# Feed-forward up projections of a two-layer block: two of the three partial products in one 512-column matmul, the sum formed afterwards

## The reference, cut to what matters

```
def conv_ffn(h, w_up, conv_w, conv_b, w_down):
    u = h @ w_up                                   # (256, 1024) @ (1024, 8192)
    u = causal depthwise conv of u, 3 taps, + conv_b
    gate, val = jnp.split(u, 2, axis=-1)
    return (jax.nn.gelu(gate, approximate=True) * val) @ w_down
```

## Time and profile before

| what | value |
|---|---|
| median of three runs | 2301.82 us |
| the profiled execution's own time | 2301.09 us |
| its span in the trace | 2299.3 us |
| TensorE, matmuls, busy over the span | 2040.8 us, 89% |
| VectorE busy | 1628.1 us, 71% |
| ScalarE busy | 1147.3 us, 50% |

### The profile page before, as it was taken

One profiled execution on the slowest core, in us unless ns is written; L12 is line 12 of the kernel. 1 busy time (PEld: TensorE's weight loads), 2 busy tenths in 40 slices (PEclk: granted clock), 3 DMA queues, 4 the chain that ended last, 5 costly groups with the idle time before them and its releaser, 6 DMA issues.

```text
span 2299.3 us, 30590 instructions
## 1 busy us (share of the span) xinstructions
PE 2040.8 (89%) x10162; PEld 1354.8 (59%) x10162; DVE 1628.1 (71%) x3313; ACT 1147.3 (50%) x2527; POOL 850.2 (37%) x574
## 2 busy tenths in 40 slices
PE   9999999999999899987778788999899987778887
PEld 8998899998999744432223233998754432223222
DVE  4564777776776787777677776776787767677776
ACT  5454455555454555544444445455555544444453
POOL 0000011100010256566666663020265566666664
PEclk9999999999999999999999999999999999999999
DMA  7543466665535799999999999534799999999997
GB/s 245 167 127 119 138 188 203 199 188 194 178 112 178 279 421 421 421 421 421 421 421 419 422 422 370 176 120 166 266 421 421 421 421 422 421 420 422 422 422 323
DMA packets 120993, 710.39 MB, mean 309 GB/s; under 512 B 14016, under 2 KB 14272, under 8 KB 54720
## 3 DMA queue, kind: packets, MB, share of 16 engines
q0 software_dynamic: 76992, 546.34, 57.5%
q1 hardware_dynamic: 41744, 151.60, 20.5%
q10 hardware_dynamic: 2160, 11.17, 1.2%
HBM read 708.02 MB, written 4.19 MB: 310 GB/s over the span
## 4 chain that ended last, share of the span: by engine, by line
PE 43%; DMA 24%; POOL 9%; issue 8%; DVE 7%; ACT 7%; DVEq 0%; POOLq 0%; ACTq 0%
DMA work<-in_experts,expert_idx 24%; PE ps L477 10%; PE ps L478 10%; PE ps L479 10%; POOL work L988 9%; PE ps L1174 7%; PE ps L615 2%; DVE work L1865 2%; DVE weights_lo L462 2%; PE ps L593 1%; PE ps L583 1%; ACT L1461 1%; ACT weights_hi L457 1%; ACT L1407 1%; ACT arena L1466 1%
## 5 line engine op out<-in xcount | busy, mean ns | idle before, releaser
L1174 PE MATMUL ps<-work,arena 128*128 128x512 f32 x2048 | 1002.5, 623 | 216.0 <-ACT arena L1466 215.0
L988 POOL DMA_INDIRECT work<-in_experts,expert_idx x512 | 798.2, 1559 | 591.9 <-PE ps L1174 306.3
L1174 PEld LDWEIGHTS ps<-work,arena 128*128 128x128 f32 x2048 | 365.1, 193 | 828.8 <-ACT arena L1466 523.3
L1865 DVE CUSTOM_DVE_ANT_0 work<-h_norm,work 128x1024 f32<-128x1024 f32 x480 | 588.1, 1225 | 309.8 <-DMA work<-in_experts,expert_idx 305.7
L462 DVE TENSOR_TENSOR weights_lo<-weights,weights_hi 128x1024 fp32r<-128x1024 f32 x286 | 354.7, 1245 | 180.9 <-ACT weights_hi L457 179.9
L477 PE MATMUL ps<-feat_hi,weights_hi 128*128 128x256 f32 x1576 | 459.6, 292 | 9.2 <-DVE weights_lo L462 5.8
L457 ACT ACTIVATE weights_hi<-weights 128x1024 fp32r<-128x1024 f32 x286 | 301.7, 1057 | 321.9 <-PE ps L479 288.3
L1461 ACT ACTIVATE small<-small 128x1 f32<-128x1 f32 x512 | 150.2, 293 | 606.6 <-DVE small L1865 585.4
L478 PE MATMUL ps<-feat_lo,weights_hi 128*128 128x256 f32 x1576 | 446.7, 283 | 0.0
L479 PE MATMUL ps<-feat_hi,weights_lo 128*128 128x256 f32 x1576 | 446.5, 283 | 0.0
L477 PEld LDWEIGHTS ps<-feat_hi,weights_hi 128*128 128x128 f32 x1576 | 303.0, 192 | 18.6 <-issue 9.0
(11 more groups left out here) (218 smaller groups left out, 1777.5 us busy)
## 6 DMA issues: line engine op xcount, KB each, us to landing
weights<-in_wstream SPq DMA_DIRECT2D x286, 512.0 KB, 3.8
work<-in_experts,expert_idx POOLq DMA_INDIRECT x512, 14.6
arena<-in_wstream POOLq DMA_DIRECT2D x12, 512.0 KB, 6.4
na_rows<-in_rpb POOLq DMA_DIRECT2D x32, 96.0 KB, 4.6
arena<-na_rows ACTq DMA_DIRECT2D x2, 1536.0 KB, 9.9
params<-in_par ACTq DMA_DIRECT2D x2, 1476.0 KB, 6.6
arena<-in_bias ACTq DMA_DIRECT2D x5, 512.0 KB, 4.9
params<-in_par ACTq DMA_DIRECT2D x1, 1024.0 KB, 6.4
```

The costliest lines, as they stand in the source:

```text
L988: nc.gpsimd.indirect_dma_start(ring[:, r, :], None, experts, bass.IndirectOffsetOnAxis(ap=EIDX[:, b, c * RING + r:c * RING + r + 1], axis= ...
L1174: ins = nc.tensor.matmul(bank(2 * t + h), DIAG[:, r, :], ring[:, r, D + h * 512:D + (h + 1) * 512], start=False, stop=False)
L1865: nc.vector.tensor_tensor_reduce(ring[:, r, 0:D], HN[:, t, :], ring[:, r, 0:D], 1.0, 0.0, ALU.mult, ALU.add, hd[:, r:r + 1]).then_inc(dots ...
```

## The change

High and low part of a chunk of features now lie side by side in one tensor (`FEAT`, of which `FH` and `FL` are views). `block_wide` issues two matmuls for a chunk: the high part of the weights against both parts of the features, 512 columns, and the low part of the weights against the high features, 256 columns, added to the second 256 columns of the first. A half so fills a bank of its own with two sums, and two blocks use banks 4 to 7. Behind them stand two new steps: ScalarE copies the second sums of a block to SBUF (`ff_copy_act`, 128 x 512), VectorE adds the first sums (`ff_sum_dve`, 128 x 512) into the tensor `ffu` in SBUF. The taps read `ffu` in place of PSUM, and TensorE waits for `ff_summed` where it waited for `ff_conv`. Elsewhere in the program only the access patterns of the feature parts change.

```diff
-        FH, FL = sb("feat_hi", [P, KC, S], F32R), sb("feat_lo", [P, KC, S], F32R)
+        FEAT = sb("feat", [P, KC, 2, S], F32R)
+        FH, FL = FEAT[:, :, 0, :], FEAT[:, :, 1, :]
...
+        ffu = work[:, 2048:3072].rearrange("p (j g n) -> p j g n", j=2, g=2)
...
+        def ff_parts(j, a):
+            return ps[:, (4 + 2 * j) * 512:(6 + 2 * j) * 512].rearrange("p (g a n) -> p g a n", g=2, a=2)[:, :, a, :]
+
+        def block_wide(pe, g, j, at=0, also=None):
+            for h in range(2):
+                w, out = split_pe(pe, 2 * g + h, at), bank(4 + 2 * j + h)
+                for c in range(KC):
...
+                    hi, lo = cols(w, c * P, P)
+                    nc.tensor.matmul(out, hi, FEAT[:, c, :, :].rearrange("p a n -> p (a n)"), start=c == 0, stop=False)
+                    ins = nc.tensor.matmul(out[:, S:2 * S], lo, FH[:, c, :], start=False, stop=c == KC - 1)
+                ins.then_inc(half_done, 1)
...
             with pe.Fori(0, FF_BLOCKS // 2 - 1) as i:
...
-                    pe.wait_ge(ff_conv, i * 2 + j + 1)
-                    group_fm(pe, G_FF + 2 + j, 6 + j, at)
+                    pe.wait_ge(ff_summed, i * 2 + j + 1)
+                    block_wide(pe, G_FF + 2 + j, j, at)
...
+            def ff_copy_act(j, done):
+                act.wait_ge(half_done, done)
+                nc.scalar.activation(ffu[:, j, :, :], ff_parts(j, 1), ACT.Copy).then_inc(ff_copied, 1)
+
             def ff_init_act(j, cvw, done):
-                act.wait_ge(half_done, done)
+                act.wait_ge(ff_summed, done)
                 for gv in range(2):
-                    ins = nc.scalar.activation(ffacc[:, j, gv, :], bank(6 + j)[:, gv * S:(gv + 1) * S], ACT.Identity,
+                    ins = nc.scalar.activation(ffacc[:, j, gv, :], ffu[:, j, gv, :], ACT.Identity,
                                                scale=cvw(gv, 2), bias=cvw(gv, 3))
...
                     split_hi(act, F_HALF + 7 + 2 * j, at)
+                    ff_copy_act(j, at.halves + F_HALF + 6 + 2 * j)
+                    split_hi(act, F_HALF + 8 + 2 * j, at)
                     act.wait_ge(ff_prod, i * 2 + j + 1)
-                    ff_init_act(j, taps, at.halves + F_HALF + 6 + 2 * j)
-                    split_hi(act, F_HALF + 8 + 2 * j, at)
+                    ff_init_act(j, taps, i * 2 + 3 + j)
                     ff_gelu_act(i * 2 + 2 + j, j)
...
+            def ff_sum_dve(blk, j):
+                dve.wait_ge(ff_copied, blk + 1)
+                nc.vector.tensor_tensor(ffu[:, j, :, :], ff_parts(j, 0), ffu[:, j, :, :], ALU.add).then_inc(ff_summed, 1)
...
                     split_lo(dve, F_HALF + 7 + 2 * j, at)
+                    ff_sum_dve(i * 2 + 2 + j, j)
+                    split_lo(dve, F_HALF + 8 + 2 * j, at)
                     ff_conv_dve(i * 2 + 2 + j, j, taps)
-                    split_lo(dve, F_HALF + 8 + 2 * j, at)
                     ff_gate_dve(i * 2 + 2 + j, j)
```

More of the change, by code:

```diff
@@ L250, in two, with paired_cols @@
         def two(t, b):
-            return t[:, 2 * b:2 * b + 2, :].rearrange("p c n -> p (c n)")
+            return t[:, 2 * b:2 * b + 2, :]
+        def paired_cols(ap):
+            return ap.rearrange("p (c n) -> p c n", c=2)
         x0_loaded, x1_loaded, ident_loaded, const_loaded, par1_loaded, bias_loaded = sem("x0_loaded"), sem("x1_loaded"), sem("ident_loaded"), sem("const_loaded"), sem("par1_loaded"), sem("bias_loaded")
@@ L276, in build @@
         ff_squared, ff_gained = sem("ff_squared"), sem("ff_gained")
+        ff_copied, ff_summed = sem("ff_copied"), sem("ff_summed")
         ff_init, ff_conv, ff_gelu, ff_gated = sem("ff_init"), sem("ff_conv"), sem("ff_gelu"), sem("ff_gated")
@@ L369, in norm_dve_pre @@
                 if gain_fm is None:
-                    ins = nc.vector.tensor_tensor(two(FL, b), bank(b), two(FH, b), ALU.subtract)
+                    ins = nc.vector.tensor_tensor(two(FL, b), paired_cols(bank(b)), two(FH, b), ALU.subtract)
                 else:
@@ L386, in norm_act_hi @@
                 if gain_fm is None:
-                    ins = nc.scalar.activation(two(FH, b), bank(b), ACT.Copy)
+                    ins = nc.scalar.activation(two(FH, b), paired_cols(bank(b)), ACT.Copy)
                 else:
@@ L499, in group_fm @@
                                       c == chunks[0], c == chunks[-1])
+                ins.then_inc(half_done, 1)
[5 more added lines that the diff above has]
+                for c in range(KC):
+                    if also and h == 0:
+                        also(c)
+                    hi, lo = cols(w, c * P, P)
+                    nc.tensor.matmul(out, hi, FEAT[:, c, :, :].rearrange("p a n -> p (a n)"), start=c == 0, stop=False)
+                    ins = nc.tensor.matmul(out[:, S:2 * S], lo, FH[:, c, :], start=False, stop=c == KC - 1)
                 ins.then_inc(half_done, 1)
@@ L695, in heads_parts @@
                 n = fill + f
-                src = bank(6 + f if f < EARLY else 4 + n % 2)
+                src = paired_cols(bank(6 + f if f < EARLY else 4 + n % 2))
                 if eng is nc.scalar:
@@ L770, in merge @@
                 for j in range(n_br):
-                    ins = nc.vector.tensor_tensor(dst if j == 0 else tmp[:, (j - 1) * 512:j * 512], bank(b + j),
+                    ins = nc.vector.tensor_tensor(dst if j == 0 else paired_cols(tmp[:, (j - 1) * 512:j * 512]), paired_cols(bank(b + j)),
                                                   two(GT[:, KC * j:KC * (j + 1), :], g), ALU.mult)
@@ L778, in merge @@
                 for j in range(1, n_br):
-                    ins = nc.vector.tensor_tensor(dst, dst, tmp[:, (j - 1) * 512:j * 512], ALU.add)
+                    ins = nc.vector.tensor_tensor(dst, dst, paired_cols(tmp[:, (j - 1) * 512:j * 512]), ALU.add)
                     if j < n_br - 1:
@@ L1068, in _ @@
             for j in range(2):
-                group_fm(pe, G_FF + j, 6 + j, also=(lambda c: c % 2 or pe.wait_ge(n_ffn.hT, c // 2 + 1)) if j == 0 else None)
+                block_wide(pe, G_FF + j, j, also=(lambda c: c % 2 or pe.wait_ge(n_ffn.hT, c // 2 + 1)) if j == 0 else None)
             for b in range(4):
@@ L1313, in _ @@
             for j in range(2):
-                ff_init_act(j, static_taps(j), F_HALF + 2 * j + 2)
+                ff_copy_act(j, F_HALF + 2 * j + 2)
                 if j == 0:
                     split_hi(act, F_HALF + 4)
+                ff_init_act(j, static_taps(j), j + 1)
                 ff_gelu_act(j, j)
@@ L1399, in _ @@
                     act.wait_ge(n_peer.xp, 4 * l + b + 1)
-                    nc.scalar.activation(two(FH, b), bank(b), ACT.Copy).then_inc(n_peer.hi, 1)
+                    nc.scalar.activation(two(FH, b), paired_cols(bank(b)), ACT.Copy).then_inc(n_peer.hi, 1)
                     if b == 1:
@@ L1545, in ff_conv_dve @@
                         acc = ffacc[:, j, gv, back:S]
-                        ins = nc.vector.scalar_tensor_tensor(out=acc, in0=bank(6 + j)[:, gv * S:(gv + 1) * S - back], scalar=taps(gv, k),
+                        ins = nc.vector.scalar_tensor_tensor(out=acc, in0=ffu[:, j, gv, 0:S - back], scalar=taps(gv, k),
                                                              in1=acc, op0=ALU.mult, op1=ALU.add)
@@ L1569, in _ @@
             for j in range(2):
-                ff_conv_dve(j, j, static_taps(j))
+                ff_sum_dve(j, j)
                 if j == 0:
                     split_lo(dve, F_HALF + 4)
+                ff_conv_dve(j, j, static_taps(j))
                 ff_gate_dve(j, j)
@@ L1661, in lower @@
                     dve.wait_ge(n_peer.hi, 4 * l + b + 1)
-                    nc.vector.tensor_tensor(two(FL, b), bank(b), two(FH, b), ALU.subtract).then_inc(n_peer.hT, 1)
+                    nc.vector.tensor_tensor(two(FL, b), paired_cols(bank(b)), two(FH, b), ALU.subtract).then_inc(n_peer.hT, 1)
                 for g in range(WO):
```

## The result

The changed kernel takes 2310.43 us, the median of 6 runs (2309.14 to 2311.40), beside 2301.94 us for the kernel before (6 runs, 2300.79 to 2303.45). The ratio is 1.0038, 95% interval 1.0028 to 1.0048: slower by 8.5 us, past what can be told from no change. I had forecast 2308, with 0.60 on slower.

A forecast was written before the change was run, and what follows sets the result against it. TensorE was taken to bound the feed-forward part; its saving is lost to waits: loop +2.4, start +1.35, end +2.6, sum +6.3 us on 2301.09 gives 2307.4, median 0.7 above, so 2308 us; range 2301.5 to 2317.

The forecast's parts named there:

- The loop's cycle: Feed-forward loop: helpers' lists and load make a body 17.1 to 17.2 us against 16.98; +2.4 us over 14 bodies.
- T = 13.44: Time in the loop body, counted from ScalarE's start on high F+8, at which low F+11 was to end.
- released by the load: Sign in a loop body: ScalarE's high part of F+8 starts when its load lands, taken as 3.5 us.
- The two ways round the cycle: Next body's high F+8 starts at 17.16 through F+11's freed slot and load, or 17.1 through TensorE's F+11 and the copy.
- the clearly slower rival: Load for F+8 takes the median 4.3 us, not 3.5: body 17.95, whole 2318 us; chance 0.2.
- The start: Ahead of the loop and first body: TensorE waits 2.0 us for F+6; +1.35 us with that stretch's savings.
- The end: Ahead of the last down matmuls: TensorE waits 3.9 us for block 30's gated parts, 1.3 lost before; +2.6 us.
- What TensorE saves: Up halves: a chunk costs 0.348 us in place of 0.360, 6.1 us in all, 0.38 a body, matmuls needing 16.60.
- the first sign: In a loop body after the change: matmul steps of 0.228 and 0.120 us for each chunk.
- the faster: Rival: SBUF taps at 0.28 us, cycle 15.7, TensorE sets the body again; 2298 us; chance 0.08.
- the about-the-same rival: Cycle of 16.9 gives 2304.5 us, or SBUF taps at 0.42 give cycle 16.7 and 2301; chance 0.28.
- the rivals that needed cheaper taps: Faster rival (taps 0.28 us, chance 0.08) and the about-the-same rival's second form (taps 0.42, 0.1 of its 0.28).

The follow-up runs named there:

- experiment 10: Changed kernel with only the split of F+6 moved ahead of the loop, each body ending with the next body's F+6 split; 2310.17 us, ratio 1.0039 to before.
- experiment 1: Changed kernel with F+11's high part made ahead of the second block's gelu, its low part ahead of the gate product; 2303.02 us, ratio 1.0010 to before.
- experiment 3: Changed kernel with three 256-column matmuls again for all but the first chunk of a half; copy, sum and lists kept; 2308.97 us, ratio 1.0033 to before.
- Experiment 8: Wide matmuls without copy and sum, each up half grouped as eight of 512 columns, then eight of 256; 2297.76 us, ratio 0.9980 to the kernel before.
- experiment 7: Changed kernel with lists laid out anew, nothing left out: F+6 and F+11 splits and the even block's parts moved earlier; 2299.25 us, ratio 0.9989 to before.
- experiment 6: Kernel before with one loop move: VectorE makes the even block's parts ahead of the low part of F+11; 2300.77 us, ratio 0.9994 to before.
- experiment 5: Kernel before with only the side-by-side feature tensor and its access patterns; 2301.97 us, ratio 0.9999 to before.
- experiment 9: Changed kernel with lists laid out anew and each up half's matmuls grouped, eight wide then eight narrow, nothing left out; 2296.04 us, ratio 0.9985 to before.
- experiment 4: Changed kernel without copy and sum, taps reading the first sums from PSUM, lists in the order of before; 2298.14 us, ratio 0.9988 to before.
- experiment 2: Changed kernel with 16 matmuls of zeros filling TensorE's idle time ahead of the last two down halves; 2309.45 us, ratio 1.0038 to before.

## Why the prediction was right, and where it was not

**The forecast held.** The profiled execution is 8.7 us longer; 7.8 of that lie in the feed-forward part (281.98 against 274.19 us), 0.5 ahead of it and 0.4 behind, for which I have no cause. I had 6.3. My 2308 is 2.4 below the median: the three parts that I added up are right within 0.1 each, and what is missing is 1.6 of TensorE's clock and the 0.9 outside the part.

**The loop's cycle**, +2.4: measured 240.04 from the first to the last group of down matmuls against 14 x 16.98 = 237.72, so **+2.3**, with a period of 17.15 as predicted (17.1 to 17.2). My hand-laid order puts low F+11's end at T = 13.44; it is 437.53 - 424.11 = 13.42. The load behind it landed 3.5 us on, and copy and load are then nearly level: high F+8 follows the copy 0.59 later (440.67 to 441.26), and over the whole part the load released it twice only. So "released by the load" was wrong in the letter. The two ways round the cycle, 17.16 and 17.1, were too near to each other to name one, and the clearly slower rival (4.3 for the load) did not occur.

**The start**, +1.35: from the part's first matmul to the first down matmul 25.47 against 24.09 us, **+1.4**, with the wait of 2.0 that I had. What I had not seen is that this price is not separate from the loop's: experiment 10 took the wait away, and two thirds of it came back later in the loop, most of that within the next period.

**The end**, +2.6: 3.8 us lost against 1.3, **+2.5**. Behind it **+1.6** at the low clock, which my sum lacked: it gave TensorE's clock after the long wait no term. The four add up to the 7.8, and this one is the whole distance from my 6.3 within the part. In the executions with this wait unfilled the clock fell in three of four (after idle times of 3.66 us in the changed kernel, 2.38 in experiment 1 and 3.46 in experiment 3), but not in the fourth (3.70, experiment 10). Ahead of the same matmuls the kernel before is idle 1.15 us, and its clock stays up. What decides it stays open.

**What TensorE saves**, 0.012 a chunk and 6.1 in all, is the term of the sum that was mis-sized. It is 0.007 (0.353 against 0.360), and 2.9 us over the loop where I had 5.7, since steps of 0.228 and 0.120, each read where its width stands alone, became 0.2355 and 0.117 when the widths alternate. So the first sign that I had named for a body after, steps of 0.228 and 0.120, did not come. Experiment 8, in which each width stands in a row of eight, gives both prices back. That the forecast didn't suffer is luck: the lists bound the body at 17.15 and hid it. At 16.60 TensorE would have waited 0.55, at 16.79 it waits 0.35. But the forms of the faster and the about-the-same rival in which TensorE sets the pace again were priced some 2 to 3 us too low by it.

**Copy, sum, taps.** Groups by line and shape, in the whole span:

```profile
L1329 ACT ACTIVATE work<-work,params 128x256 f32<-128x256 f32 x64 | 35.0, 594 | 11.8 <-DVE work L1573 11.7
L1581 DVE SCALAR_TENSOR_TENSOR work<-work,params 128x255 f32<-128x255 f32 x64 | 28.1, 481 | 5.9 <-ACT work L1329 5.8
...
L1573 DVE TENSOR_TENSOR work<-ps,work 128x512 f32<-128x512 f32 x32 | 22.0, 687 | 2.9 <-ACT work L1323 2.0
L1323 ACT ACTIVATE work<-ps 128x512 f32<-128x512 f32 x32 | 18.8, 588 | 31.9 <-PE ps L522 31.9
```

The sum takes 687 ns and the copy 588, near the 0.69 and 0.60 us of the prediction. Four taps of VectorE take 1.90 us from SBUF and 1.89 from PSUM, so the rivals that needed cheaper taps fell. The newest tap's pair takes 1.09 (1.02 before, 1.05 predicted). The Trainium skill (page VectorE: DVE Perf Modes, section on the TRN2 errata) would have VectorE's taps 65 ns cheaper each, by the prediction's estimate, and 481 ns in SBUF show nothing of that; its other half, ScalarE dearer from SBUF, by about 0.04 each in the estimate of the prediction, is borne out by 0.035 (half of 1.09 - 1.02), where I had taken less than half of it: I gave the pair of instructions together the 0.03 us that one pair of rows shows for a single one.

## What to carry to other kernels

When a change trades time of the bounding engine for work on its helpers, write out the helpers' lists before adding it: here L is 269.9 us as the change laid them and 258.2 as experiment 7 did, with the same instructions. Of these 11.7 us, 1.6 are the low clock behind the long wait, and about 1.2 are an order that the kernel before had already (experiment 6). A wait taken away at a loop's front can come back in the next bodies: of 2.1 us, 0.7 were left here (experiment 10). And take the step of a matmul from rows in which its neighbours are the ones it will have; here mixed widths were cheaper in groups.

## What the runs showed of the hardware

- Matmuls of 512 and 256 columns that alternate take 0.2355 + 0.117 us, eight of each in a row 0.348 a pair, a difference of 0.005 for each pair (0.15 us on 32 pairs). Three of 256 with changing stationary tensors cost 0.120 each, so it is not the change of `weights_hi` and `weights_lo`; why the change of width costs, no run shows.
- The down halves, the same instructions everywhere, take 5.47 us in most bodies before and in experiments 5, 6, 8 and 9, 5.50 in experiments 1, 3, 4 and 7, and 5.45 to 5.48 in the changed kernel and experiment 2. I can name no cause for it.
- TensorE's clock at the feed-forward part's first matmuls is not the same from one execution to the next. Over 280 to 284 us the granted clock is 1.00 in the kernel before and 0.74 in experiment 6, whose code is the same up to the loop. There the first matmul lies 13.25 us ahead of the loop's start, in place of 12.40. The row is that of experiment 6:

```profile
280.00:284.00 4.00, 3.27 (x20) 2.90 (x21) 1.99 (x6) 3.25 (x9) 0.00 (x0) 0.74 0.00 0
```
